# Gates and branches of two hybrid layers with the weights as the moving operand, and five places where work is reordered

## The chip, the cores and the metric

One core of a Trainium2 chip runs the whole program in one launch. The metric is the device time in microseconds (us) of one execution, as a median of several runs. Lower is better.

## What is computed

256 tokens of width 1024 go through a first block (mixer with attention, a recurrent unit and a memory; then a layer of 16,384 experts) and through two hybrid layers. All weights are float32. The part of a hybrid layer that the change rewrites is this:

```python
h = rms_norm(x, norm1_g)
z = h @ w_in
za, zb, zc, zd, zg = jnp.split(z, IN_SPLITS, axis=-1)
ya = retention(za, ret_gn_g)
yb = conformer_conv(zb, conv_w, conv_b, conv_ln_g, conv_ln_b)
yc = spatial_gating(zc, gmlp_ln_g, gmlp_ln_b, gmlp_ws, gmlp_bs)
yd = swa_attention(zd, swa_q_g, swa_k_g, swa_sinks, rel_bias)
ys = jnp.stack([ya, yb, yc, yd], axis=2)
branches = jnp.einsum('bsnc,ncd->bsnd', ys, w_branch)      # 4 branches, 512 -> 1024
gates = jax.nn.sigmoid(zg.reshape(B, S, 4, D_MODEL))       # 1024 -> 4096
mix = jnp.sum(gates * branches, axis=2)
x = x + mix @ w_out
```

## The kernel before

**Stream of weights.** Every weight matrix is cut into units of 512 KB (128 partitions x 1024 float32). SyncE loads them in one fixed order into three raw slots. For each unit ScalarE makes a rounded high half (`hi`, L1181) and GpSimd (two halves of 512 columns, L2606) or VectorE (L1777) makes the remainder, the low half. In most of the program seven units of eight are GpSimd's; in the expert layer's second half, around `w_out` and in the feed-forward VectorE makes all. Four split slots hold the results, so `hi` of unit n may start when TensorE is done with unit n-4. A float32 product is three TensorE passes: high x high, high x low, low x high (`mm3`, L568 to L570).

**Two forms of a unit.** `fm_unit` (L601) gives features by tokens: the weights are the stationary operand (128x128) and the 256 tokens move, so a unit is 24 matmuls of 128x256. `tm_unit` (L628) gives tokens by features: 128 tokens are stationary and 512 weight columns move, so a unit is 12 matmuls of 128x512. The gates and branches are `fm_unit`, `w_out` is `tm_unit`.

**PSUM.** Eight banks: three stream banks that `fm_unit` takes in rotation, and five side banks (`SIDE` is 3) for everything else.

**Order.** Each engine's program is written in rounds: a `main` generator yields once per unit, and after each of its steps the `sides` (convolution, spatial gating, retention, window attention) are stepped once, in the order of a list. Each engine executes its instructions in order. In a hybrid layer `main` does the projections, the 32 gate units, then 16 branch units in the branch order 0, 1, 3, 2, then `project_out` with the 8 units of `w_out`. While gates run, the convolution's normalisation, the spatial gating, and the eight window heads are done on VectorE and ScalarE between them. The sums over branches (L2530, L2531) lie in `gates2`, features by tokens, which is the layout `w_out` needs for its stationary operand: ScalarE and VectorE make its high and low halves (`mix_hi` L1228, `mix_lo` L1830) straight from `gates2`.

**Expert layer.** 128 units of `peer_u` produce one row of expert activations each; 128 units of `peer_v` use them, each with a high and low half of one expert row (`expert_pair`, three of them in rotation, in the space of `h2T`). So that `h2T` is free, the first pair waits for the last `peer_u` matmul. SyncE reloads the residual `X` in four pieces between the first loads of `peer_v`.

**Start.** The memory's values `vm` (4 units, `tm_unit`) use two side banks, which the normalisation of x uses too: its transposes (L689) alternate with the units.

Of the kernel before, what the change touches and what calls it, by code (L numbers as in the profile page):

```python
# [265 lines left out]
class Kernel:  # L266
# [130 lines left out]

    def peer_tiles(self, phase):
# [10 lines left out]
        self.epair = [self.pair(f"expert_pair{i}", [P, TOKENS], at=hot + i * 2048) for i in range(3)]  # L409
        self.g_final = self.place("g_final", [P, D], at=hot + 8192)  # L410
# [30 lines left out]
    def layer_tiles(self, phase):  # L441
# [26 lines left out]
        self.gates2 = self.place("gates2", [P, 32, TOKENS])  # L468
# [82 lines left out]
def pe_program(k):  # L551
# [76 lines left out]
    def tm_unit(key, i, lhs, first, chunks, width, banks, start, stop, ready=None):  # L628
# [5 lines left out]
        for c in range(chunks):  # L634
            if ready is not None:
                pe.wait_ge(*ready(first + c))
            for t, h in ends:
                last = mm3(banks[t][h][:, 0:wd], lhs.at(lambda x: x[:, first + c, t * P:(t + 1) * P]),
# [12 lines left out]
    def close_banks(key, units, lhs_of, ready_of, banks):  # L651
# [19 lines left out]
        at.unit = U[key, units - 1] + 1  # L671

# [44 lines left out]
    def token_major(key, units, chunks, width, lhs, ready=None):  # L717
        banks = [[take(SIDE + t, (key, t))] for t in range(TILES)]
# [32 lines left out]
    def project_out(key, lhs, ready, turns=iter(())):  # L751

        for half in range(2):
            banks = [[take(SIDE + 2 * half + t, (key, half, t))] for t in range(TILES)]
            for u in range(4):
                tm_unit(key, half * 4 + u, lhs, 2 * u, 2, 512, banks, u == 0, u == 3, ready if half == 0 else None)
                if half == 1 and u in (1, 2):
                    next(turns, None)
# [11 lines left out]
    def mixer():  # L770
# [78 lines left out]
        def main():  # L849
# [5 lines left out]
            yield from token_major("vm", 4, 2, 512, k.memT)  # L855
# [30 lines left out]
    def peer():  # L886
# [47 lines left out]
        pe.wait_ge(k.sem("unit_gated"), units_gated(KEYS - 1))  # L934
        for j in range(KEYS - CLOSING):
            ep = k.epair[j % 3]
            pe.wait_ge(k.sem("expert_lo"), j + 1)
            one = ep.at(lambda x: x[:, :].unsqueeze(1))
            tm_unit("peer_v", j, one, 0, 1, 1024, banks, j == 0, False)
        close_banks("peer_v", KEYS, lambda j: k.epair[j % 3], lambda j: (k.sem("expert_lo"), j + 1), banks)  # L940

    def layer(l):
# [17 lines left out]
        def convolution():  # L960
# [24 lines left out]
            for i in range(KM):  # L985
# [12 lines left out]
        def gating():  # L998
            while not at.reached(name("gu"), KM - 1) or name("conv_stats") not in at.stages:
                yield  # L1000
            for i in range(KM):
# [10 lines left out]
                last.then_inc(k.sem("gating_mm"), 1)  # L1012
                yield
# [73 lines left out]

        def main():
# [1886 lines left out]
```

## Time and profile before

| | us |
|---|---|
| median of 3 runs (2141.98 to 2144.8) | 2142.35 |
| the profiled execution's own time | 2145.49 |
| its span, first to last instruction | 2144.2 |
| TensorE busy | 2113.1 (99%) |
| weight loads of TensorE busy | 1958.1 (91%) |
| VectorE / ScalarE / GpSimd busy | 1395.7 / 1247.4 / 977.1 |
| mean granted TensorE clock | 0.998 of full speed |

Around the span lie 1.3 us (2145.49 less 2144.2). TensorE's busy times overlap each other, because matmuls are pipelined: a matmul's own duration is longer than the distance to the next one. The distance between starts is the cost.

### The profile page before, as it was taken

Reading aid. Unit: us, or ns where it says so; the run is one execution under the profiler, and the core shown is the slowest. Engines: PE = TensorE matmul, PEld = TensorE weight load, DVE = VectorE, ACT = ScalarE, POOL = GpSimd, SP = SyncE. Lnnn points to the kernel's source line nnn. Section 1 sums busy time; section 2 is a strip of 40 time slices with the busy share of each in tenths; the row PEclk is TensorE's granted clock in tenths of the full one; section 3 lists DMA queues with packets and bytes.
Section 4 is the critical chain, followed back from the end, with each engine's and each line's share of the span. In section 5 each row is a group of like instructions: output and inputs, shape, how many; then the busy total and the mean of one; then the engine's idle time right before and its main releaser. Section 6 shows DMA issues by size and latency. Waiting matters only on the chain.

```text
span 2144.2 us, 37243 instructions
## 1 busy us (share of the span) xinstructions
PE 2113.1 (99%) x14292; PEld 1958.1 (91%) x14292; DVE 1395.7 (65%) x2706; ACT 1247.4 (58%) x2272; POOL 977.1 (46%) x791
## 2 busy tenths in 40 slices
PE   7999999999999999999999999999999999999999
PEld 7999989999999998888889899998888999998887
DVE  4467655998676756666667765557764864757874
ACT  5669454546777865455445465746555465756553
POOL 4776557999667650000004785660001876661000
PEclk9999999999999999999999999999999999999999
DMA  6444565655444456666665554555565645455565
GB/s 231 149 138 129 172 197 173 196 178 180 145 140 147 141 168 204 195 192 192 195 195 196 186 157 139 155 180 167 187 205 158 189 146 168 141 165 177 187 194 160
DMA packets 103952, 370.59 MB, mean 173 GB/s; under 512 B 11480, under 2 KB 12896, under 8 KB 103264
## 3 DMA queue, kind: packets, MB, share of 16 engines
q1 hardware_dynamic: 103776, 368.21, 54.8%
q8 instruction: 115, 1.88, 0.4%
q14 instruction: 61, 0.50, 0.1%
HBM read 366.05 MB, written 2.11 MB: 172 GB/s over the span
## 4 chain that ended last, share of the span: by engine, by line
PE 88%; DVE 6%; ACT 2%; POOL 1%; issue 1%; DMA 1%; SPq 0%; DVEq 0%; ACTq 0%; POOLq 0%
PE stream_bank L568 14%; PE stream_bank L570 14%; PE stream_bank L569 14%; PE side_bank L568 9%; PE side_bank L570 9%; PE side_bank L569 9%; PE side_bank L577 4%; PE stream_bank L577 4%; PE side_bank L574 2%; PE stream_bank L574 2%; PE side_bank L918 1%; PE side_bank L917 1%; POOL unit_lo L2606 1%; ACT unit_hi L1181 1%; PE side_bank L746 1%
## 5 line engine op out<-in xcount | busy, mean ns | idle before, releaser
L2606 POOL TENSOR_TENSOR unit_lo<-raw,unit_hi 128x512 fp32r<-128x512 f32 (+1 forms) x724 | 938.5, 1324 | 943.6 <-ACT unit_hi L1181 941.6
L1181 ACT ACTIVATE unit_hi<-raw 128x1024 fp32r<-128x1024 f32 (+1 forms) x678 | 708.9, 1046 | 199.5 <-PE side_bank L570 66.0
L1777 DVE TENSOR_TENSOR unit_lo<-raw,unit_hi 128x1024 fp32r<-128x1024 f32 (+1 forms) x316 | 390.3, 1236 | 227.9 <-ACT unit_hi L1181 225.9
L568 PE MATMUL stream_bank<-hT,unit_hi 128*128 128x256 f32 x1360 | 398.9, 293 | 1.8 <-POOL unit_lo L2606 1.8
L570 PE MATMUL stream_bank<-hT,unit_lo 128*128 128x256 f32 x1360 | 384.6, 283 | 0.0
L569 PE MATMUL stream_bank<-hT,unit_hi 128*128 128x256 f32 x1360 | 384.5, 283 | 0.0
L568 PE MATMUL stream_bank<-h2T,unit_hi 128*128 128x256 f32 x1024 | 293.3, 286 | 0.0
L570 PE MATMUL stream_bank<-h2T,unit_lo 128*128 128x256 f32 x1024 | 289.8, 283 | 0.0
L569 PE MATMUL stream_bank<-h2T,unit_hi 128*128 128x256 f32 x1024 | 289.6, 283 | 0.0
L568 PEld LDWEIGHTS stream_bank<-hT,unit_hi 128*128 128x128 f32 x1360 | 259.9, 191 | 3.6 <-POOL unit_lo L2606 2.0
L569 PEld LDWEIGHTS stream_bank<-hT,unit_hi 128*128 128x128 f32 x1360 | 260.0, 191 | 1.6
L570 PEld LDWEIGHTS stream_bank<-hT,unit_lo 128*128 128x128 f32 x1360 | 259.8, 191 | 0.0
L568 PE MATMUL side_bank<-unit_hi,expert_pair 128*128 128x512 f32 x512 | 200.0, 391 | 2.1 <-DVE experts L2238 2.1
L569 PE MATMUL side_bank<-unit_lo,expert_pair 128*128 128x512 f32 x512 | 199.8, 390 | 0.0
L570 PE MATMUL side_bank<-unit_hi,expert_pair 128*128 128x512 f32 x512 | 199.7, 390 | 0.0
L568 PEld LDWEIGHTS stream_bank<-h2T,unit_hi 128*128 128x128 f32 x1024 | 196.6, 192 | 0.0
L569 PEld LDWEIGHTS stream_bank<-h2T,unit_hi 128*128 128x128 f32 x1024 | 196.6, 192 | 0.0
L570 PEld LDWEIGHTS stream_bank<-h2T,unit_lo 128*128 128x128 f32 x1024 | 196.3, 192 | 0.0
L1228 ACT ACTIVATE expert_pair<-experts 128x256 fp32r<-128x256 f32 x128 | 53.4, 418 | 173.3 <-PE side_bank L570 170.8
L577 PE MATMUL side_bank<-sumT,unit_hi 128*128 128x512 f32 x384 | 134.1, 397 | 0.2
L2318 DVE SCALAR_TENSOR_TENSOR side_bank<-conv_in,cols,side_bank 128x256 f32<-128x256 f32 x232 | 113.2, 488 | 6.9
L568 PEld LDWEIGHTS side_bank<-unit_hi,expert_pair 128*128 128x128 f32 x512 | 96.5, 188 | 22.4 <-issue 2.2
(392 smaller groups left out, 4303.9 us busy)
## 6 DMA issues: line engine op xcount, KB each, us to landing
raw<-in_peer_u_dram SPq DMA_DIRECT2D x128, 512.0 KB, 3.5
raw<-in_peer_v_dram SPq DMA_DIRECT2D x128, 512.0 KB, 4.1
raw<-in_gate_dram SPq DMA_DIRECT2D x64, 512.0 KB, 3.5
raw<-in_gt_dram SPq DMA_DIRECT2D x44, 512.0 KB, 3.5
raw<-in_up_dram SPq DMA_DIRECT2D x44, 512.0 KB, 3.5
raw<-in_ffn_out_dram SPq DMA_DIRECT2D x44, 512.0 KB, 3.5
raw<-in_branch_dram SPq DMA_DIRECT2D x32, 512.0 KB, 3.5
raw<-in_w_gate_dram SPq DMA_DIRECT2D x24, 512.0 KB, 3.5
```

The source lines that it names most:

```text
L568: mm(out, l.hi, r.hi, start=start, stop=False)
L569: mm(out, l.hi, r.lo, start=False, stop=False)
L570: return mm(out, l.lo, r.hi, start=False, stop=stop)
L574: low = lambda: mm(bank[:, 0:TOKENS], w.lo, r.hi[:, c, :], start=False, stop=False, skip_group_check=True)
L577: last = mm(bank[:, :].rearrange("p (a t) -> p a t", a=2), w.hi, r.both[:, :, c, :], start=start, stop=stop, skip_group_check=True)
L746: last = mm(bank[:, a:a + n], s.v(kt), s.PT[:, kt * TOKENS + a:kt * TOKENS + a + n], start=(i == 0), stop=(i == len(order) - 1), skip_grou ...
L917: mm(out, first[:, j, :], second[:, j, 0, :], start=True, stop=False)
L1181: activation(k.unit_hi[n % SPLIT_SLOTS][:, 0:w], k.raw[n % RAW_SLOTS][:, 0:w], ACT.Copy).then_inc(k.sem("unit_hi"), 1)
L1228: activation(dst, src, ACT.Copy, scale=scale).then_inc(k.sem(sem), 1)
L1777: V.tensor_tensor(k.unit_lo[s][:, 0:w], k.raw[n % RAW_SLOTS][:, 0:w], k.unit_hi[s][:, 0:w], ALU.subtract).then_inc(unit_lo, 1)
L2318: own.then(V.scalar_tensor_tensor(sums, k.cu[:, i, j:j + TOKENS], w(j), sums, ALU.mult, ALU.add))
L2606: last = G.tensor_tensor(k.unit_lo[s][:, cols], k.raw[n % RAW_SLOTS][:, cols], k.unit_hi[s][:, cols], ALU.subtract)
```

## The change

It does six things; line numbers of the changed kernel are some 100 higher.

1. Gates and branches become `block_unit`: activations stationary, 512 weight columns moving. A block (4 gate units, 2 branch units) fills two stream banks, one for each 128 tokens. ScalarE evicts each bank of a gate block once, 128x512; `add_branch` adds each half branch with the same two VectorE instructions per bank as before.
2. The sums are now tokens by features, so `turn_merged` transposes them on TensorE (16 transposes of 128x128 a layer, in two groups of 8: inside the last branch and behind the first unit of `w_out`), and ScalarE and VectorE make the halves from PSUM (`merged_hi`, `merged_lo`).
3. In the layers VectorE's retention steps come ahead of the convolution's in each round, the window heads last.
4. The convolution's low halves are put two rounds later, and the gating's steps are three rounds apart, not two.
5. `vm` takes stream banks.
6. The first expert pair lies in the space of `X`, so it does not wait for the last `peer_u` matmul; TensorE waits for the last expert's gate only ahead of the second half of `peer_v` unit 0; the reload of `X` waits for `peer_v` unit 0.

```diff
+    def block_unit(key, block, units, u, lhs, banks):
+        i = block * units + u
+        n = U[key, i]
+        w = unit(n)
+        for t in range(TILES):
+            if u == 0:
+                banks.append(take(rotation[turn[0] % len(rotation)], (key, "block", block, t)))
+                turn[0] += 1
+            for c in range(2):
+                last = mm3(banks[t][:, :], lhs.at(lambda x: x[:, 2 * u + c, t * P:(t + 1) * P]),
+                           w.at(lambda x: x[:, c * 512:(c + 1) * 512]), u == 0 and c == 0, u == units - 1 and c == 1)
...
+    def turn_merged(label, x, half, ready):
+        for k2 in (2 * half, 2 * half + 1):
+            bank = take(SIDE + 2 + k2 % 2, (label, k2))
...
+                for t in range(TILES):
+                    last = nc.tensor.transpose(bank[:, j * TOKENS + t * P:j * TOKENS + (t + 1) * P],
+                                               x[:, t, c * P:(c + 1) * P], k.ident)
...
-            yield from token_major("vm", 4, 2, 512, k.memT)
+            yield from token_major("vm", 4, 2, 512, k.memT, in_stream=True)
...
-        pe.wait_ge(k.sem("unit_gated"), units_gated(KEYS - 1))
         for j in range(KEYS - CLOSING):
-            ep = k.epair[j % 3]
+            ep = k.expert_pair(j)
...
+            late = (k.sem("unit_gated"), units_gated(KEYS - 1)) if j == 0 else None
...
-            for i in range(32):
-                fm_unit(name("gate"), i, k.hT2, KD)
-                yield
+            for block in range(8):
+                banks = []
+                for u in range(4):
+                    block_unit(name("gate"), block, 4, u, k.hT2, banks)
+                    yield
...
-                for i in range(KD // 2):
-                    fm_unit(name("branch"), n * KD // 2 + i, part, KM, 2)
-                    yield
+                for half in range(2):
+                    banks = []
+                    for u in range(2):
+                        block_unit(name("branch"), 2 * n + half, 2, u, part, banks)
+                        if n == BRANCH_ORDER[-1] and half and u == 0:
+                            turn_merged(name("merged"), merged, 0, summed())
+                        yield
...
         def expert_hi(j):
             if j == 0:
-                act.wait_ge(unit_mm, U["peer_u", KEYS - 1] + 1)
+                act.wait_ge(k.sem("gates_mm"), 2 * GROUPS)
                 act.wait_ge(*k.over["gates", GROUPS - 1])
             if j == 1:
+                act.wait_ge(unit_mm, U["peer_u", KEYS - 1] + 1)
...
-        at.run(main(), [bias_tables() if l == 0 else iter(()), own_channels(), sides()])
+        at.run(main(), [bias_tables() if l == 0 else iter(()), at.finished(name("branch0"), retention()),
+                        own_channels(), window_heads()])
...
     sp.wait_ge(k.sem("landed_x_out"), 16 * 2 * TILES)
+    sp.wait_ge(k.sem("unit_mm"), U["peer_v", 0] + 1)
```

VectorE in the first hybrid layer, at the first retention head's normalisation, before. `conv_in` rows are taps of the convolution, `ret_n` is what TensorE's transposes at L1056 wait for.

```order
L2425 TENSOR_SCALAR smalls_52<-smalls_52 128x2 [waits dve_own]
L2318 SCALAR_TENSOR_TENSOR side_bank<-conv_in_144,cols_49,side_bank 128x256
L2318 SCALAR_TENSOR_TENSOR side_bank<-conv_in_144,cols_49,side_bank 128x256 [waits dve_own] x3
L1777 TENSOR_TENSOR unit_lo_14_62<-raw_7_55,unit_hi_10_58 128x1024 [waits unit_hi,dve_own]
L2318 SCALAR_TENSOR_TENSOR side_bank<-conv_in_144,cols_49,side_bank 128x256
L2318 SCALAR_TENSOR_TENSOR side_bank<-conv_in_144,cols_49,side_bank 128x256 [waits dve_own] x3
L2431 RECIPROCAL smalls_52<-smalls_52 128x2 [waits ret_root,dve_own]
L2433 TENSOR_SCALAR ret_n_160<-side_bank,smalls_52 128x128 [waits dve_own]
L2433 TENSOR_SCALAR ret_n_160<-side_bank,smalls_52 128x128
L2410 TENSOR_TENSOR S_105_153<-side_bank,layer_consts_134 128x256 [waits ret_scored]
L2411 TENSOR_TENSOR S_105_153<-side_bank,layer_consts_134 128x128
```

The same place of the changed kernel.

```order
L2507 TENSOR_SCALAR smalls_52<-smalls_52 128x2 [waits dve_own]
L2394 SCALAR_TENSOR_TENSOR side_bank<-conv_in_145,cols_49,side_bank 128x256
L2394 SCALAR_TENSOR_TENSOR side_bank<-conv_in_145,cols_49,side_bank 128x256 [waits dve_own] x7
L1851 TENSOR_TENSOR unit_lo_14_62<-raw_7_55,unit_hi_10_58 128x1024 [waits unit_hi,dve_own]
L2513 RECIPROCAL smalls_52<-smalls_52 128x2 [waits ret_root]
L2515 TENSOR_SCALAR ret_n_161<-side_bank,smalls_52 128x128 [waits dve_own]
L2515 TENSOR_SCALAR ret_n_161<-side_bank,smalls_52 128x128
L2492 TENSOR_TENSOR S_106_154<-side_bank,layer_consts_135 128x256 [waits ret_scored]
L2493 TENSOR_TENSOR S_106_154<-side_bank,layer_consts_135 128x128
```

Of the eight taps that stood on both sides of the low half of a weight unit, all now stand ahead of it, and nothing stands between it and the `ret_n` rows.

TensorE at the end of the last branch and the beginning of `w_out`, before (`ys` are the branches' inputs, `hT` the merged rows' halves).

```order
L568 MATMUL stream_bank<-ys_139,unit_hi_13_61 128x256
L569 MATMUL stream_bank<-ys_139,unit_hi_13_61 128x256
L570 MATMUL stream_bank<-ys_139,unit_lo_17_65 128x256
L568 MATMUL stream_bank<-ys_139,unit_hi_13_61 128x256
L569 MATMUL stream_bank<-ys_139,unit_hi_13_61 128x256
L570 MATMUL stream_bank<-ys_139,unit_lo_17_65 128x256
L568 MATMUL side_bank<-unit_hi_10_58,hT_88_136 128x512 [waits unit_lo_pool,mix_lo,bank_free4,bank_free3]
L569 MATMUL side_bank<-unit_lo_14_62,hT_88_136 128x512
L570 MATMUL side_bank<-unit_hi_10_58,hT_88_136 128x512
```

The first unit of `w_out` in the changed kernel, from its seventh matmul on, and the second group of transposes (`gates` are the merged rows, L708 is in `turn_merged`).

```order
L572 MATMUL side_bank<-unit_hi_10_58,hT_89_137 128x512 [waits bank_free5]
L573 MATMUL side_bank<-unit_lo_14_62,hT_89_137 128x512
L574 MATMUL side_bank<-unit_hi_10_58,hT_89_137 128x512
L572 MATMUL side_bank<-unit_hi_10_58,hT_89_137 128x512
L573 MATMUL side_bank<-unit_lo_14_62,hT_89_137 128x512
L574 MATMUL side_bank<-unit_hi_10_58,hT_89_137 128x512
L708 MATMUL side_bank<-base_consts_50,gates_104_152 128x128 [waits bank_free2,bank_free1,bank_free5]
L708 MATMUL side_bank<-base_consts_50,gates_104_152 128x128 x3
L708 MATMUL side_bank<-base_consts_50,gates_104_152 128x128 [waits bank_free2,bank_free1,bank_free6]
L708 MATMUL side_bank<-base_consts_50,gates_104_152 128x128 x3
L572 MATMUL side_bank<-unit_hi_11_59,hT_89_137 128x512 [waits bank_free6,unit_lo_pool]
L573 MATMUL side_bank<-unit_lo_15_63,hT_89_137 128x512
```

Before, `w_out` follows the branch with no other matmul between; now eight transposes stand behind its first unit, and they wait for the sums of the last half branch (bank_free1, bank_free2) and for the low halves made from the first group (bank_free5, bank_free6).

SyncE at the first loads of `peer_v` (raw) and the reload of X, before.

```order
L2747 DMA raw_8_56<-in_peer_v_dram 128x1024 [waits unit_lo_pool]
L2747 DMA raw_9_57<-in_peer_v_dram 128x1024 [waits unit_lo_pool]
L2757 DMA X_53<-x_scratch 128x512 [waits landed_x_out,gates_mm]
L2747 DMA raw_7_55<-in_peer_v_dram 128x1024 [waits unit_lo_pool]
L2757 DMA X_53<-x_scratch 128x512
L2747 DMA raw_8_56<-in_peer_v_dram 128x1024 [waits unit_lo_pool]
```

The same of the changed kernel.

```order
L2846 DMA raw_8_56<-in_peer_v_dram 128x1024 [waits unit_lo_pool]
L2846 DMA raw_9_57<-in_peer_v_dram 128x1024 [waits unit_lo_pool]
L2856 DMA X_53<-x_scratch 128x512 [waits unit_mm,landed_x_out,gates_mm]
L2846 DMA raw_7_55<-in_peer_v_dram 128x1024 [waits unit_lo_pool]
L2856 DMA X_53<-x_scratch 128x512
L2846 DMA raw_8_56<-in_peer_v_dram 128x1024 [waits unit_lo_pool]
```

The order is the same; the first reload of X has one more wait (unit_mm), and the load of the fifth unit of `peer_v` stands right behind it.

## Rows read from the trace of the kernel before

**Rows 1.** Page, part 1: busy us (share of span) xinstructions of each engine

```profile
PE 2113.1 (99%) x14292; PEld 1958.1 (91%) x14292; DVE 1395.7 (65%) x2706; ACT 1247.4 (58%) x2272; POOL 977.1 (46%) x791
```

**Rows 2.** Waits of TensorE: who for whom, us in total, times, longest

```profile
PE side_bank L1056 <- DVE S L2411: 2.9, 2, 1.4
...
PE side_bank L1008 <- DVE gmlp_u L2377: 2.1, 2, 1.1
PE side_bank L568 <- DVE experts L2238: 2.1, 1, 2.1
PE side_bank L568 <- issue: 1.9, 1, 1.9
PE side_bank L728 <- issue: 1.6, 2, 0.8
PE side_bank L568 <- ACT vm L1372: 1.5, 1, 1.5
```

**Rows 3.** Timeline of TensorE, last branch and `w_out`: start, us

```profile
1403.84 0.36 PE L568 MATMUL stream_bank<-ys,unit_hi 128*128 128x256 f32 x1
...
1432.71 0.40 PE L568 MATMUL side_bank<-unit_hi,hT 128*128 128x512 f32 x1
...
1449.07 0.60 PE L691 MATMUL side_bank<-base_consts,X 128*128 128x128 f32 x4
...
1452.27 0.60 PE L691 MATMUL side_bank<-base_consts,X 128*128 128x128 f32 x4
```

**Rows 4.** Timeline of VectorE in the branches

```profile
1418.58 0.69 DVE L2530 SCALAR_TENSOR_TENSOR stream_bank<-gates,stream_bank 128x512 f32<-128x512 f32 x1 [1.53 <-PE stream_bank L570]
1419.31 0.69 DVE L2531 TENSOR_TENSOR gates<-gates,stream_bank 128x512 f32<-128x512 f32 x1
```

**Rows 5.** Timeline of ScalarE in the branches

```profile
1425.79 0.63 ACT L1228 ACTIVATE hT<-gates 128x512 fp32r<-128x512 f32 x1 [3.28 <-DVE gates L2531]
```

**Rows 6.** GpSimd's groups with their shapes, gates and branches of layer 0

```profile
L2606 POOL TENSOR_TENSOR unit_lo<-raw,unit_hi 128x512 fp32r<-128x512 f32 x76 | 98.1, 1315 | 51.9 <-ACT unit_hi L1181 51.6
```

**Rows 7.** Timeline of VectorE around the first retention head

```profile
1221.30 1.23 DVE L1777 TENSOR_TENSOR unit_lo<-raw,unit_hi 128x1024 fp32r<-128x1024 f32 x1 [3.40 <-ACT unit_hi L1181]
1222.44 2.06 DVE L2318 SCALAR_TENSOR_TENSOR side_bank<-conv_in,cols,side_bank 128x256 f32<-128x256 f32 x4
...
1225.72 0.28 DVE L2411 TENSOR_TENSOR S<-side_bank,layer_consts 128x128 f32<-128x128 f32 x1
```

**Rows 8.** Timeline of TensorE at the same place

```profile
1226.05 0.44 PE L1056 MATMUL side_bank<-base_consts,ret_n 128*128 128x128 f32 x2 [1.44 <-DVE S L2411]
```

**Rows 9.** Timeline of VectorE in the gates, first and last of its unbroken stretch

```profile
1318.26 1.75 DVE L2341 RECIPROCAL t2b<-t2b 128x256 f32<-128x256 f32 x1 [7.46 <-ACT t2b L1564]
...
1342.93 0.41 DVE L2377 TENSOR_TENSOR gmlp_u<-side_bank,gmlp_u 128x256 f32<-128x256 f32 x1
```

**Rows 10.** Timeline of TensorE at the start

```profile
30.89 0.47 PE L568 MATMUL side_bank<-unit_hi,memT 128*128 128x512 f32 x1 [1.89 <-issue]
...
69.08 0.39 PE L568 MATMUL stream_bank<-hT,unit_hi 128*128 128x256 f32 x1 [1.76 <-POOL unit_lo L2606]
```

**Rows 11.** Timeline of VectorE at the start

```profile
41.80 0.27 DVE L1942 MEMSET rope_s<- 128x256 f32 x1
```

**Rows 12.** Windows: stretch, its us, busy (instructions) of PE, PEld, DVE, ACT, POOL, PEclk, DMA share, GB/s

```profile
31.50:35.00 3.50, 3.50 (x10) 2.72 (x9) 0.00 (x0) 0.00 (x0) 2.56 (x3) 0.51 0.98 342
...
789.20:792.70 3.50, 3.43 (x8) 2.78 (x9) 1.98 (x3) 1.41 (x3) 0.00 (x0) 0.51 0.75 228
```

**Rows 13.** Timeline of TensorE at the start of `peer_v`

```profile
789.27 0.77 PE L568 MATMUL side_bank<-unit_hi,expert_pair 128*128 128x512 f32 x1 [2.05 <-DVE experts L2238]
```

**Rows 14.** Timeline of SyncE's issues there: start, us to issue

```profile
785.48 0.33 SPq L2747 DMA_DIRECT2D raw<-in_peer_v_dram  x1
```

**Rows 15.** Page, part 6: DMA issues, KB each, median us to landing

```profile
raw<-in_peer_v_dram SPq DMA_DIRECT2D x128, 512.0 KB, 4.1
```

**Rows 16.** Page, part 5: ScalarE's high halves, all of the program

```profile
L1181 ACT ACTIVATE unit_hi<-raw 128x1024 fp32r<-128x1024 f32 (+1 forms) x678 | 708.9, 1046 | 199.5 <-PE side_bank L570 66.0
```

More of the change, by code:

```diff
@@ L626, in halves_unit, with tm_unit @@
         at.unit = n + 1
-    def tm_unit(key, i, lhs, first, chunks, width, banks, start, stop, ready=None):
+    def tm_unit(key, i, lhs, first, chunks, width, banks, start, stop, ready=None, late=None):
         n = U[key, i]
@@ L715, in chunks_of, with token_major @@
         return lambda c: k.over[name, c // 2]
-    def token_major(key, units, chunks, width, lhs, ready=None):
-        banks = [[take(SIDE + t, (key, t))] for t in range(TILES)]
+    def token_major(key, units, chunks, width, lhs, ready=None, in_stream=False):
+        if in_stream:
+            banks = [[take(rotation[(turn[0] + t) % len(rotation)], (key, t))] for t in range(TILES)]
+            turn[0] += TILES
+        else:
+            banks = [[take(SIDE + t, (key, t))] for t in range(TILES)]
         for u in range(units):
@@ L984, in convolution @@
             yield
[L985 removed]
+            for i in range(KM + 1):
                 yield
@@ L1086, in swa @@
                 head(s, [(k.sem("swa_scaled"), 5 * l + 2 + s.column), k.over[name("sv"), 1]]) for s in heads])
+        merged = k.gates2[:, :, BRANCH_ORDER[0] * D:(BRANCH_ORDER[0] + 1) * D]
+        last_branch = lambda half, t: (name("branch"), "block", 2 * BRANCH_ORDER[-1] + half, t)
+        summed = lambda: {2 * h + t: k.over[last_branch(h, t)] for h in range(2) for t in range(TILES)
+                          if last_branch(h, t) in k.over}
         def main():
@@ L1691, in main @@
             for i in range(32):
-                evict(name("gate"), i, k.gates2[:, i, :], ACT.Tanh, scale=0.5)
+                advance(name("gate"), i)
+                if i % 4 == 3:
+                    for t in range(TILES):
+                        label = (name("gate"), "block", i // 4, t)
+                        act.wait_ge(*k.mm_done[label])
+                        activation(k.gates2[:, t, i // 4 * 512:(i // 4 + 1) * 512], k.bank[k.bank_of[label]][:, :], ACT.Tanh,
+                                   scale=0.5).then_inc(k.free[k.bank_of[label]], 1)
                 yield
@@ L1872, in add_out @@
                 advance(key, half * 4 + u)
+                if half == 0 and u == 0 and behind_first is not None:
+                    behind_first()
                 if half == 1 and u in (1, 2):
@@ new lines, in main, with add_branch @@
+                for i in range(KD // 2):
+                    advance(name("branch"), n * KD // 2 + i)
+                    if i % 2:
+                        add_branch(place, n, i // 2)
+                    yield
+        def add_branch(place, n, half):
+            for t in range(TILES):
+                if place == BRANCHES2 - 1 and half:
+                    merged_lo(t)
+                label = (name("branch"), "block", 2 * n + half, t)
+                b = k.bank_of[label]
+                bank = k.bank[b][:, :]
+                gate = k.gates2[:, t, n * D + half * 512:n * D + (half + 1) * 512]
+                first = BRANCH_ORDER[0] * D + half * 512
+                total = k.gates2[:, t, first:first + 512]
+                if place == 0:
+                    dve.wait_ge(*k.over[name("gate"), "block", 2 * n + half, t])
+                dve.wait_ge(*k.mm_done[label])
+                if place == 0:
+                    V.scalar_tensor_tensor(gate, gate, 1.0, bank, ALU.add, ALU.mult).then_inc(k.free[b], 1)
+                    dve.wait_ge(*k.over[label])
+                else:
+                    own.then(V.scalar_tensor_tensor(bank, gate, 1.0, bank, ALU.add, ALU.mult))
+                    V.tensor_tensor(total, total, bank, ALU.add).then_inc(k.free[b], 1)
+                    dve.wait_ge(*k.over[label])
```

114 lines of the change are left out of this document (69 added, 45 removed).

## The prediction

> **What bounds the kernel now.** I read the page first: TensorE is busy 99% of the span, VectorE 65%, ScalarE 58%, GpSimd 46% [rows 1]. So a change pays by what it takes off TensorE's own sequence, or by a wait of TensorE that it removes. The waits of TensorE are few, and six of its lines lie at places that the diff touches: together 12.1 us [rows 2]. Then the timeline, for the distance between starts. A matmul's own duration cannot be summed, since they overlap.
>
> **Gates and branches.** Between the two starts at 1403.84 and 1432.71 us stand 10 branch units, 240 matmuls of 128x256, with nothing between: 28.87 us, 120.3 ns each, 2.887 us a unit. From there to 1449.07 stand six units of w_out, 72 matmuls of 128x512: 16.36 us, 227.2 ns each, 2.727 us a unit [rows 3]. So one matmul of 512 columns costs 13.4 ns less than two of 256. A layer has 48 gate and branch units, so 1152 matmuls of 128x256 become 576 of 128x512. For two layers 2304 x 120.3 ns = 277.2 us becomes 1152 x 227.2 ns = 261.7 us: **-15.4 us**. The six units of w_out are exactly the new form (activations stationary, 512 weight columns moving), so I take the row as it is. Its weakness: there VectorE made the low halves of the weights, here mostly GpSimd.
>
> The Trainium skill ("TensorE: Matmul & The Clock Gate", section "Back-to-back issue gap") would make this term smaller. It gives the isolated gap of a warm matmul as its columns at 2.4 GHz plus about 2.5 ns. By that two of 256 against one of 512 differ by one fixed cost, about 2.6 ns with its rounding, and the term would be an estimated -3.0 us. The distances 120.3 and 227.2 ns of this trace are both larger than the page's 109 and 216, the first by more, so the trace does not agree with it, and the sum goes by the trace. The same section's sustained 131 ns for 512 columns isn't seen here either.
>
> What must keep up at 2.727 us a unit: GpSimd's low halves take 2 x 1.315 = 2.63 us a unit, and it waited 51.9 us in the gates and branches of one layer for the high halves [rows 6], which follow TensorE's pace. Seven units in eight are its own, so it needs 2.30 us per unit on average. It is hidden, with three units made ahead as cushion. The eviction of gates and the sums of branches come in lumps: two banks of three are held by a block, and the next block needs the third at once, the first of the two half a unit after the block's end. The sums take 0.69 + 0.69 us a bank [rows 4]; a bank's first half is complete 1.36 us before the other, so they end some 0.1 and 1.5 us after the block, and the freed banks are asked for 1.4 and 5.5 us after it. I cost this at nothing; if the cover were gone, it would be up to 1.4 us for each of 16 half branches.
>
> **Transposes of the merged rows.** Four groups of 8 over both layers. Four transposes in w_out stretch the unit after 1449.07 to 3.20 us (start of one L691 to the next) against 2.73, so 0.47 for four, 0.94 for eight [rows 3]: **+3.8 us**. The second group waits for the last sums. Call A the end of the last branch's first half. Its second half ends at A + 2 x 2.73 + 0.94 = A + 6.4, the first w_out unit at A + 9.1. VectorE has from A + 5.0 on (first bank full) two sums of 1.4 and two `merged_lo` of about 0.7 (as rows 4), which makes A + 9.0 if the first of them starts at A + 4.8; ScalarE's halves are 0.63 each [rows 5]. That is only 0.1 under the point where TensorE arrives, so I put 0.3 a layer: **+0.6 us**. Bounds 0 and 2 x 1.4 (one sum late).
>
> **Retention ahead of the convolution.** TensorE waits 1.44 us in each layer at L1056 for VectorE [rows 2, 8]. VectorE had stood idle for 3.40 us, made a weight unit's low half, then four taps in 2.06 us, and only then the `ret_n` rows and the score products that TensorE waited for, until 1226.0 [rows 7]. The changed order has all taps ahead of the low half, in what was idle. Without the four taps VectorE is done 2.06 earlier, at 1223.9, ahead of TensorE's arrival (1226.05 - 1.44 = 1224.6), so the wait goes: -2.9, and some 0.1 of restart at each: **-3.1 us**. Bounds: 0 (taps late in their turn delay another step) and -3.2.
>
> **Convolution and gating steps.** The two waits at L728 and L1008 are 1.6 + 2.1 = 3.7 us for both layers [rows 2]. VectorE works without a break from 1318.26 to 1343.34 [rows 9], after 7.46 us in which it waited for ScalarE's square root. The edit changes the order in that stretch, not its 25 us of work, and by its end TensorE will have done 11 gate units that are each 0.16 us shorter, so it comes 1.75 us sooner. What VectorE orders first (the window heads' queries) comes in time; the gating products at the end then come late. I think that the first wait goes and the second grows to nearly what both were: **-0.5 us**. Bounds: -3.7 when both go, and +3.5 when TensorE's 1.75 us are given back in each layer.
>
> **vm in stream banks.** The wait of 1.89 us before vm's second step is for a bank that the normalisation's halves still hold [rows 10]; in stream banks it goes. Behind it the granted clock was at the lower of its two levels (1.2 GHz) for 3.5 us, after TensorE had stood: 10 matmuls there, against 3.5 / 0.227 = 15 at the upper one, so 3.5 - 2.27 = 1.2 us [rows 12]. It shouldn't fall without the gap. Then the wait for the eviction of vm (1.5 us, rows 2) goes too, since va's banks are free. But 20 us later TensorE waits 1.76 us for a low half of GpSimd [rows 10], and GpSimd had been held up by small operations that hang on VectorE's rope tables from 41.80 on [rows 11]. That chain begins behind the last normalisation step, which moves only by the 1.9 + 1.2 us ahead of it. What TensorE gains beyond it is waited out at 69 us: **-3.1 us**. Bounds: -1.9 and -4.6 (with the 1.5).
>
> **First expert pair.** TensorE waits 2.05 us at 789.27 for VectorE [rows 13], in a chain from the last `peer_u` matmul by ScalarE's and VectorE's halves. The changed kernel makes the first pair before that matmul. The clock behind it was at the lower level as well: 8 matmuls in 3.5 us instead of 1.82 [rows 12]. 2.05 + 1.68 = **-3.7 us**. The price is on SyncE: the reload of X waits for `peer_v` unit 0 (789.27 - 2.05 + 2.73 = 789.9), and the load of the fifth unit, issued at 785.48 before [rows 14], stands behind it. Issued at 790.3 and landing 4.1 us later [rows 15] it is there at 794.4; high and low half take 1.05 [rows 16] and 1.23 [rows 7], so 796.7; TensorE needs it at 787.2 + 4 x 2.73 = 798.1. I cost it at nothing, with 1.4 us of cover; bounds of the whole part 0 and -3.8.
>
> **Sum.** -15.4 + 3.8 + 0.6 - 3.1 - 0.5 - 3.1 - 3.7 = -21.4 us. The profiled execution took 2145.49, 3.1 over the median, and would take 2124.1; the median 2142.35 becomes **2121 us**.
>
> **Rivals.**
> - The waits in the gates all vanish and vm's reach their full bound: -3.2 - 1.5 more, 2116. For it: VectorE stands idle for 7.46 us ahead of its stretch, and the square root that opens it stood behind an eviction of a gate that comes only every fourth unit now. Against: VectorE's unbroken 25 us [rows 9]. 0.15.
> - VectorE is the bound in the gates and takes back what TensorE gains there: +4 to +8, 2125 to 2129. For it: the same row, and the window heads that follow in the same queue. Against: behind that stretch TensorE has enough gates left that no side waits. 0.14.
> - The reload of X doesn't hide: landing takes longer with two more transfers beside it, and TensorE waits for `peer_v`'s fifth unit; a wait of 2 to 4 us, perhaps with the clock falling again: 2124 to 2127. Against: 1.4 us of cover. 0.06.
> - The form of the matmul gives little: 13.4 ns is a matter of where w_out's and the branches' operands lie, and the gap follows a fixed cost per instruction of some 2 to 3 ns: the term is -3, the time 2133. This is the Trainium skill's rule above. Against it stand both distances in one trace, 0.2 us apart in place. 0.03.
> - Slower. GpSimd becomes the bound of the 96 gate and branch units: with 7 of 8 units its own, the gain of 21.4 us (0.223 a unit) is gone when a unit takes 2.95 us, that is 3.37 for a unit of GpSimd, 1.69 a half against the 1.315 shown. At 1.8 a half: 3.15 a unit, +40 for the two layers, 2162. For it: evictions and sums now come in lumps beside it. Against: a mean of 1.315 over 76 instructions amid the same VectorE work [rows 6]. 0.04.
>
> **How the numbers follow.** The forecast itself has 0.58; its own range, by its bounds, is 2117 to 2125. The range **2112 to 2131** takes in the first three rivals and leaves out the last two and the ends of some bounds. A measurement tells 0.2%, 4.3 us, from no change. All cases but the last are faster by more than that; a bit of it goes to no change, where several bounds meet: faster 0.93, same 0.03, slower 0.04.
>
> **What would show it.** Right: a gate or branch unit at 2.73 us; 16 transposes a layer, with no wait over 0.5 at the second group; no wait at the `ret_n` transposes; TensorE's clock at the upper level at 31 and 788 us; `peer_v` starting within 0.2 us of the last `peer_u` matmul; one wait of 1 to 2 us left in each layer's gates, at a window head's transposes or the gating's products; a wait for GpSimd left near 65 us. Wrong: a distance of 235 ns or more between 512-column matmuls, TensorE waiting for `unit_lo` of GpSimd in many gate units, or for stream banks at the blocks' beginnings, or for the raw slot of the fifth `peer_v` unit.

## The result and the profile after

Median of four runs 2128.29 us (2126.46 to 2128.98) against 2143.57 of before (four runs): ratio 0.9926, 95% interval 0.9913 to 0.9939, 15.3 us faster. Five more runs of the same kernel (experiment `again`) gave 2129.81, so that all nine have a median of 2128.7. Forecast were 2121 and 21.4 us. The two profiled executions differ by 19.0 us, 2126.46 against 2145.49 us, and the spans as well:

The page of the changed kernel, its first lines (compare [rows 1]):

```profile
span 2125.2 us, 34923 instructions
PE 2100.6 (99%) x13172; PEld 1898.4 (89%) x13172; DVE 1394.9 (66%) x2706; ACT 1244.3 (59%) x2240; POOL 979.4 (46%) x791
```

TensorE has 1120 instructions less (1152 fewer matmuls, 32 transposes more) and is busy as before. Its waits, against [rows 2]:

```profile
PE stream_bank L572 <- POOL unit_lo L2705: 5.2, 5, 2.2
PE side_bank L780 <- ACT S L1305: 4.7, 2, 2.3
...
PE side_bank L572 <- DVE first_expert_pair L2320: 0.4, 1, 0.4
```

The six lines that the diff touched are gone from this list, but for 0.4 us at the first pair. In their place stand two new ones: 2.3 us in each layer at the transposes of the first window head (L780), and a longer wait for GpSimd's low halves at the start.

The form, on TensorE's timeline at the end of the last branch (compare [rows 3]):

```profile
1390.24 0.47 PE L572 MATMUL stream_bank<-unit_hi,ys 128*128 128x512 f32 x1
...
1414.93 1.03 PE L708 MATMUL side_bank<-base_consts,gates 128*128 128x128 f32 x8
1415.72 0.49 PE L572 MATMUL stream_bank<-unit_hi,ys 128*128 128x512 f32 x1
1416.05 0.40 PE L573 MATMUL stream_bank<-unit_lo,ys 128*128 128x512 f32 x1
...
1418.59 0.39 PE L572 MATMUL side_bank<-unit_hi,hT 128*128 128x512 f32 x1
...
1421.32 1.03 PE L708 MATMUL side_bank<-base_consts,gates 128*128 128x128 f32 x8
1422.11 0.48 PE L572 MATMUL side_bank<-unit_hi,hT 128*128 128x512 f32 x1
```

From 1390.24 to 1414.93 stand nine branch units with nothing between: 24.69 us, 2.74 a unit, with one restart in it. The undisturbed w_out unit from 1418.59 to 1421.32 takes 2.73 us. A group of eight transposes takes 0.79 us to the next start, and the unit behind it 2.87 (1415.72 to 1418.59) instead of 2.73: 0.93 a group. No row has a wait at the second group.

From the starts of the stages in both timelines (layer 0; the differences of layer 1 agree within 0.04 us):

| stage | before | after | difference |
|---|---|---|---|
| layer's norm to the first gate unit | 126.79 | 124.84 | -1.95 |
| 32 gates, with heads and gating between | 113.52 | 109.79 | -3.73 |
| 16 branch units (after: with one group of transposes) | 49.17 | 47.98 | -1.19 |
| w_out | 22.76 | 23.62 | +0.86 |

That is 6.0 us a layer, and 11.8 from the first layer's norm to the end of the second layer. The start up to the unit of 69.08 / 64.16 us gave 4.9 (1.1 of it in the first transfers, which have nothing to do with the change), the first pair 1.7 and the clock behind it 1.6; some 0.9 are lost again between 64 and 780 us.

### The profile page after: what moved, and what is told of

Read it like the earlier page. It is cut to its first block, busy times and chain, and to the rows that moved or that the text cites. A ratio compares the mean times of both kernels' runs of the same rounds, so it can differ in the third digit from the quotient of the medians.

```text
span 2125.2 us, 34923 instructions
## 1 busy us (share of the span) xinstructions
PE 2100.6 (99%) x13172; PEld 1898.4 (89%) x13172; DVE 1394.9 (66%) x2706; ACT 1244.3 (59%) x2240; POOL 979.4 (46%) x791
## 4 chain that ended last, share of the span: by engine, by line
PE 89%; DVE 6%; ACT 2%; POOL 1%; DMA 1%; issue 1%; SPq 0%; ACTq 0%; DVEq 0%; POOLq 0%
PE stream_bank L572 14%; PE stream_bank L574 14%; PE stream_bank L573 14%; PE side_bank L572 9%; PE side_bank L574 9%; PE side_bank L573 9%; PE side_bank L581 4%; PE stream_bank L581 4%; PE side_bank L578 2%; PE stream_bank L578 2%; PE side_bank L963 1%; PE side_bank L962 1%; POOL unit_lo L2705 1%; PE side_bank L789 1%; ACT unit_hi L1239 1%
## 5 line engine op out<-in xcount | busy, mean ns | idle before, releaser
L572 PE MATMUL stream_bank<-hT,unit_hi 128*128 128x256 f32 x848 | 248.6, 293 | 3.1 <-POOL unit_lo L2705 3.1
L574 PE MATMUL stream_bank<-hT,unit_lo 128*128 128x256 f32 x848 | 239.8, 283 | 0.0
L573 PE MATMUL stream_bank<-hT,unit_hi 128*128 128x256 f32 x848 | 239.7, 283 | 0.0
L572 PE MATMUL side_bank<-unit_hi,expert_pair 128*128 128x512 f32 x508 | 197.7, 389 | 0.0
L574 PE MATMUL side_bank<-unit_hi,expert_pair 128*128 128x512 f32 x508 | 197.7, 389 | 0.0
L572 PEld LDWEIGHTS stream_bank<-hT,unit_hi 128*128 128x128 f32 x848 | 162.3, 191 | 4.5 <-POOL unit_lo L2705 3.5
L573 PEld LDWEIGHTS stream_bank<-hT,unit_hi 128*128 128x128 f32 x848 | 162.3, 191 | 0.9
L574 PEld LDWEIGHTS stream_bank<-hT,unit_lo 128*128 128x128 f32 x848 | 162.2, 191 | 0.0
```

What stands on the lines that cost most here:

```text
L572: mm(out, l.hi, r.hi, start=start, stop=False)
L573: mm(out, l.hi, r.lo, start=False, stop=False)
L574: return mm(out, l.lo, r.hi, start=False, stop=stop)
```

## The experiments

Differences to the changed kernel are to its median of nine runs, 2128.7. `again` repeats it. The nine lie between 2126.5 and 2131.2, so a difference of 2 to 3 us between two medians is hardly clear of the noise. The stages of the profiles tell more. Here is the time from the first gate unit's start to the first branch unit's, in us; a star marks a layer in which the granted clock fell to its lower level in this stage.

| kernel | layer 0 | layer 1 |
|---|---|---|
| changed kernel | 109.79 | 109.78 |
| again | 109.79 | 111.32* |
| form_only | 111.31* | 111.42* |
| steps_undone | 109.81 | 111.15* |
| act_heads_first | 114.52* | 113.85* |
| turn_later (branches 1.9 longer) | 108.73 | 108.75 |
| pool_gates | 109.12 | 109.09 |
| gating_late | 108.50 | 108.50 |

**again.** 

> The changed kernel unaltered, run again beside before. The timed medians differ by 15.3 us, the two profiled executions by 19.0. If the profile of the changed kernel was merely a quick execution, the difference comes out at 15 to 17 us again and the new profile's span lies 1 to 2.5 us above 2125.2, with the excess in places that do not belong to the change (the first transfers, waits for a transfer). If the profile is typical and the timed runs were not, it comes out at 18 to 20.

2129.81 us (2126.9 to 2131.15), ratio 0.9937 (0.9924 to 0.9951); before 2143.47 in 16 runs. The difference was 15.3 us in the first comparison and is 13.7 here, under both ranges expected; and this profile is again of a quick execution, 2126.9 us. The 19.0 of the two profiles came of an execution 1.8 us under its median beside one 2 to 3 over its own. Where executions differ is shown below under the clock.

**form_only.** The retention order, the convolution and gating steps, vm's banks and the first pair as before.

> Only the 512-column form and the transposes that it needs; the other four changes (retention order, convolution and gating steps, vm's banks, first expert pair) are undone. By the terms of the prediction 15.4 - 3.8 - 0.6, so 11 us faster than before. By the stages of the two profiles (gates -3.75, branches -1.2, w_out +0.9 in a layer) only about 8. Where VectorE bounds the gates, 7.5 or less, and the waits in the gates grow over the 3.7 us of before.

2137.36 us (ratio 0.9975, 0.9966 to 0.9984): 6.1 faster than before, where the terms said 11. Its waits of TensorE in the gates:

```profile
PE stream_bank L572 <- ACT gates L1756: 5.1, 2, 2.6
```

ScalarE ahead of that wait's end (1333.29), in layer 0:

```profile
1330.76 0.60 ACT L1628 ACTIVATE conv_out<-conv_out,cols 128x256 f32<-128x256 f32 x1 [1.96 <-DVE conv_out L2418]
...
1332.66 1.06 ACT L1756 ACTIVATE gates<-stream_bank 128x512 f32<-128x512 f32 x2
```

The row of TensorE is a wait that I had costed at nothing, "evictions come in lumps": the next block's bank waits for ScalarE to evict a gate block, and ScalarE, in order, stands at work that VectorE has not yet released. It is 2.6 us a layer where before had 0.8 and 1.0 [rows 2]. That makes 1.4 of the 5 us that are missing; 3 are restarts, counted below. In the profile the clock fell behind this wait in both layers; how much of the rest that is can't be read from one profile.

**steps_undone.** Only the convolution's and the gating's steps as before:

```diff
-            for i in range(KM + 1):
+            for i in range(KM):
                 yield
...
                 last.then_inc(k.sem("gating_mm"), 1)
                 yield
                 yield
-                yield
```

and the matching steps on ScalarE and VectorE. 

> The changed kernel with the convolution's and the gating's steps as before. If the stretch is bounded by VectorE's 25 us of work, the order matters little: within 1.5 us of the changed kernel, with waits of 3 to 6 us over both layers left at the heads' transposes or the gating. If these steps were what removed the two waits of before, it is 3.7 us slower. If they are what made the new wait of 2.3 us a layer, it is 2 to 4 us faster.

2131.08 us, 2.4 slower, but its five runs (2126.3 to 2132.33) take in all nine of the changed kernel, so the time shows no difference. The eviction's wait of 2.6 us a layer is back and the 2.3 at the transposes is gone: one wait for another of like size. The gates of layer 0 take 109.81 us against 109.79, so the steps are worth nothing; in layer 1, and near 64 us, the clock fell.

**act_heads_first.**

```diff
-        at.run(main(), [bias_tables() if l == 0 else iter(()), own_channels(), sides()])
+        at.run(main(), [bias_tables() if l == 0 else iter(()), sides(), own_channels()])
```

on ScalarE. 

> The changed kernel with ScalarE stepping the window heads ahead of the convolution and gating in each round. In the profile the wait of 2.3 us a layer at the first head's transposes ends with ScalarE's normalisation of that head, which stands behind the rounding of the gating's first product, itself waiting for VectorE; the head's reciprocal was ready 2.6 us earlier. If the order on ScalarE is the cause, the wait shrinks to about 1.1 and the kernel is 2.4 us faster than the changed one. If VectorE bounds the stretch, the wait reappears at the gating or the next head and the time stays.

2136.56 us, 7.9 slower. Both theories fell: the wait grew to 3.5 us a layer, and one of 0.7 came before it at the scores. Together that is 3.6 us more for both layers; in the profile, 10.6 us longer than the changed kernel's, the clock also fell behind both waits and near 64 us. From TensorE's waits in this kernel (line, for whom, us in total, times, longest):

```profile
PE side_bank L780 <- ACT S L1305: 6.9, 2, 3.5
...
PE side_bank L771 <- issue: 1.4, 2, 0.7
```

**turn_later.**

```diff
-        for _ in range(5):
+        for _ in range(5 if s.bias is None else 6):
             yield
```

on TensorE, with a step more on ScalarE and VectorE. 

> The changed kernel with the transposes of each window head, and what follows from them, one round later on TensorE, ScalarE and VectorE. If the wait of 2.3 us a layer is only the first head's normalisation coming one round late, it goes: 4.7 to 5 us faster than the changed kernel, and up to 2.5 more in executions in which the clock would have fallen behind these waits, so 2122 to 2124. If VectorE's and ScalarE's work bounds the stretch, a wait of about the same length comes back at the next head or the gating or a stream bank, and the time stays within 1.5 us of 2128.7.

2129.39 us, no gain. The wait at L780 went, and 2.0 us for GpSimd's low half and 1.0 us for VectorE's branch sums came in each layer. The gates end 1.1 us sooner, the branches take 1.9 longer. So four orders of the same work leave 2.3 to 4.2 us of waits a layer. None ends them, which points to VectorE and ScalarE as the bound there; but the order is not indifferent, as `act_heads_first` and `gating_late` show.

**vm_side.**

```diff
-            yield from token_major("vm", 4, 2, 512, k.memT, in_stream=True)
+            yield from token_major("vm", 4, 2, 512, k.memT)
```

> The changed kernel with vm in the side banks again. If vm's new banks gave the 3.8 us that the two profiles show up to 64 us, this is 3 to 4 us slower than the changed kernel's 2128.7 (median of its nine runs). If what TensorE gained there is waited out at the low halves of GpSimd, which hang on VectorE's tables, the wait near 64 us (2.2 in the changed kernel) is 0.5 or so shorter here and the loss is 2 us or less. If the clock falls behind the gap of 1.9 us in only some executions, runs differ by about 1.4 us and the loss has two levels.

2131.05 us (2129.8 to 2135.6), 2.3 slower. The gap of 1.89 us is back at 30.62 and the wait near 68 is 1.73 (2.17 in the changed kernel): between the two theories. In the profile, of the slowest execution, the clock fell behind the gap, and 3.8 us are lost between 20 and 70 us.

**pair_undone.** The first expert pair in `h2T`'s space, its waits and SyncE's as before. 

> The changed kernel with the first expert pair made as before. The gap of 2.05 us at the start of peer_v comes back for the 0.4 of the changed kernel: 1.7 us slower where the clock stays up behind the gap, 3.2 where it falls as in the profile of before. The prediction had 3.7.

2133.37 us, 4.7 slower, more than either figure expected; the gap of 2.06 is back. In the profile the clock fell behind it, and the two cost 3.2 us between 780 and 800 us.

**dve_order.** VectorE's convolution steps ahead of the retention's. 

> The changed kernel with VectorE's convolution steps ahead of the retention's again. The wait at the ret_n transposes comes back: 1.6 us a layer with the restart, and 0.2 at the next head, 3.1 to 3.9 us in all, unless the order in the gates changes with it, which can give or take 2 us.

2133.95 us, 5.2 slower, over the 3.9 expected. By the profile the retention costs 1.94 us more in each layer, 3.9 in both. TensorE's waits in this kernel have the row of [rows 2] again, with the same size:

```profile
PE side_bank L1102 <- DVE S L2493: 2.9, 2, 1.4
```

**later_spread.** turn_later, and in GpSimd's `tables`:

```diff
-                if i % 3 == 0:
-                    yield
+                yield
```

> As turn_later, and GpSimd's small table operations in the first stage one pair a round instead of three, so that the low halves near 58 and 64 us come in time. If these operations are what the two waits there hang on (1.0 and 2.2 us in the changed kernel), 2 to 3.5 us faster than turn_later. If the transfers or the normalisation's chain bound that stretch, within 1 us of turn_later.

2128.78 us, 0.6 faster than turn_later, within the noise. The waits at 58 and 64 us shrank from 1.0 and 2.3 to 0.3 and nothing, 3.0 us at 108 us, but waits for low halves at 240 to 290 us took half back: 1.3 were left at 348 us.

**pool_gates.** In the assignment of the low halves:

```diff
+            if any(U[f"gate.{l}", 0] + 8 <= n < U[f"gate.{l}", 0] + 28 for l in range(LAYERS)):
+                by = "pool"
```

> The changed kernel with the low halves of gate units 8 to 27 all on GpSimd, so that VectorE loses one of 1.22 us inside its unbroken stretch in each layer. If VectorE's amount of work sets the wait at the first head's transposes, it falls from 2.3 to 1.1 us a layer, the clock no longer falls behind it, and the kernel is 2.4 to 4 us faster than the changed one (2128.7). If GpSimd's additional work slows VectorE's products of two SBUF operands (0.42 us alone, 1.4 to 1.5 beside GpSimd in the profile), the wait stays over 2 us.

2126.26 us (2125.64 to 2127.23), 2.4 faster. The wait fell from 2.34 to 1.70 us a layer, about half of the 1.22 us that one low half takes VectorE; that is 1.3 us for both layers, and where the rest of the 2.4 lies is not shown. VectorE's stretch from the first reciprocal to the gating product became only 0.68 us shorter, 27.49 us (1307.36 to 1334.85) against 28.17 (1305.18 to 1333.35). Rows of this kernel, VectorE's timeline and then GpSimd's at the same time:

```profile
1321.77 1.52 DVE L2428 TENSOR_TENSOR ys<-conv_out,ys 128x256 fp32r<-128x256 f32 x1
...
1324.98 0.99 DVE L2544 SCALAR_TENSOR_TENSOR swa_q<-swa_q,cols,swa_var 128x256 f32<-128x256 f32 x1
...
1327.33 0.41 DVE L2428 TENSOR_TENSOR ys<-conv_out,ys 128x256 fp32r<-128x256 f32 x1
```

```profile
1321.45 5.67 POOL L2707 TENSOR_TENSOR unit_lo<-raw,unit_hi 128x512 fp32r<-128x512 f32 x4 [0.96 <-ACT unit_hi L1241]
1333.61 2.53 POOL L2707 TENSOR_TENSOR unit_lo<-raw,unit_hi 128x512 fp32r<-128x512 f32 x2 [6.48 <-ACT unit_hi L1241]
```

The same product takes 1.52 us while GpSimd makes low halves (until 1327.12) and 0.41 behind them, while GpSimd does nothing. The changed kernel has the 1.5 and the 0.4 at other products, with no net change; but the scaling at 1324.98 took 0.55 there, and those 0.44 us are most of what is missing. GpSimd was at work beside it in both kernels. Its low half and the scaling, first in the changed kernel, then in this one (the third of the four):

```profile
1322.92 1.29 POOL L2705 TENSOR_TENSOR unit_lo<-raw,unit_hi 128x512 fp32r<-128x512 f32 x1 [0.96 <-ACT unit_hi L1239]
1323.95 0.55 DVE L2542 SCALAR_TENSOR_TENSOR swa_q<-swa_q,cols,swa_var 128x256 f32<-128x256 f32 x1
```

```profile
1324.41 1.29 POOL L2707 TENSOR_TENSOR unit_lo<-raw,unit_hi 128x512 fp32r<-128x512 f32 x1
1324.98 0.99 DVE L2544 SCALAR_TENSOR_TENSOR swa_q<-swa_q,cols,swa_var 128x256 f32<-128x256 f32 x1
```

In both the scaling ends 0.3 us behind the low half; here it began earlier in it. So VectorE pays for the rest of GpSimd's running instruction, and the price hangs on where in it the product begins. That GpSimd's additional work brought the worse place is argued, not shown. The Trainium skill ("GPSIMD Engine Reference", "Specifications") says that the SBUF interfaces are shared with VectorE, with contention for instructions of two SBUF inputs; the trace agrees, and gives the price.

**pool_spread.** pool_gates with the spread tables. 

> As pool_gates, with GpSimd's table operations spread at the start as in later_spread, which ended the two waits near 58 and 64 us there (3.5 us, of which 1.3 were left at 348 us). Expected 1 to 3 us faster than pool_gates, with no wait over 1.5 us between 20 us and the end and no lower clock behind one.

2122.98 us (2120.8 to 2123.84, four runs), ratio to before 0.9901 (0.9886 to 0.9916): 5.7 faster than the changed kernel and 3.3 faster than pool_gates, and the best here; in its profile the clock fell nowhere from 20 us to the end. Of the waits of TensorE, 1.7 us a layer are left at the window head, more than the expectation had, and up to 1.2 for low halves:

```profile
PE side_bank L782 <- ACT S L1307: 3.4, 2, 1.7
PE stream_bank L574 <- POOL unit_lo L2707: 3.0, 4, 1.2
```

**gating_late.** pool_spread with a step moved from behind `gating_hi` on ScalarE, and from behind `gating_lo` on VectorE, to ahead of it. 

> As pool_spread, and the rounding of each gating product on ScalarE (and its low half on VectorE) one round later, so that the first head's normalisation no longer stands behind it. In pool_spread the wait of 1.70 us a layer ends with that normalisation, which starts 0.3 us behind the rounding of a product that VectorE had just made, while the head's reciprocal was 2.6 us old. If that order on ScalarE is what is left, the wait falls to about 0.6 us a layer: 2 us faster than pool_spread (2123.0), so 2121. If VectorE's work is what is left, the wait moves to another instruction and the time stays within 1 us.

2123.21 us, the same within the noise. The wait at L782 fell to 0.47 us as expected, 0.4 of the gain came back as a wait for a low half one unit later, and there was another of 1.4 us in the first block, which the edit does not touch. The gates take 108.50 us for pool_spread's 109.1, so 1.2 us are gained in both layers; the first block lost 0.7 of them in this profile. TensorE's waits:

```profile
PE stream_bank L574 <- DVE gates L2184: 1.4, 1, 1.4
...
PE side_bank L782 <- ACT S L1307: 0.9, 2, 0.5
```

## Why the prediction held, and which terms were off

The direction, the range and the main term's mechanism held; the size was 6 to 8 us off, the worth of three terms (1, 4 and 7). The time lies outside the forecast's own 2117 to 2125 and among the 2125 to 2129 of the rival in which VectorE takes back 4 to 8 us. It does so by luck: the waits there grew by 0.9 us in all, and most of what is missing is in terms that the rival left alone.

1. **Gates and branches, -15.4 forecast, about -12.4 measured.** The cadence of the new form is the predicted 227 ns where nothing interrupts. The step that failed is "a gate or branch unit at 2.73 us": I priced every unit as an undisturbed one. In a layer the block units stand in 28 stretches between heads, transposes and gating products (26 before). The first unit behind such a place pays a restart: 2.87 us behind the transposes above and 2.96 behind a head's scores instead of 2.73, where before it was 2.97 and 3.06 instead of 2.89. Summed over the gates and branches of a layer, without the waits, the stretches take 5.0 us more than their matmuls at the undisturbed cadence, and 3.4 before: 1.6 us a layer, which the term lacked. The rival in which 512 columns save only a fixed cost of 2 to 3 ns is refuted: undisturbed, 12 matmuls take 2.73 us for 24 in 2.89, now in branch units as well, with the branches' operands. The rule of the Trainium skill that I weighed ("TensorE: Matmul & The Clock Gate", "Back-to-back issue gap") gives an estimated 3.0 us for this term; the trace disagrees by a factor of four.
2. **Transposes, +3.8 and +0.6.** 4 x 0.93 = 3.7, and no wait at the second group. Right.
3. **Retention, -3.1.** Stage -1.95 a layer, -3.9, and 5.2 in the timed undoing. The wait went, and so did a small one at the second head that I had left out.
4. **Convolution and gating, -0.5 forecast, +0.9 measured.** The prediction said that one of the two waits would go and the other grow to nearly the sum. It grew beyond it: 2.34 against 0.83 + 1.04 a layer. The step that failed is "the edit changes the order in that stretch, not its 25 us of work". From the first reciprocal to the first gating product VectorE took 24.67 us before [rows 9] and takes 28.17 now, in both layers; with the old steps (`form_only`, `steps_undone`) it took 24.6, so the steps did it. They put the second head's scores ahead of the gating product, and more of the products beside GpSimd's low halves (twelve products of 128x256 take 10.1 us, 8.4 before). The stretch and the end of its chain in the changed kernel, VectorE, ScalarE and TensorE one after the other:

```profile
1305.18 1.75 DVE L2417 RECIPROCAL t2b<-t2b 128x256 f32<-128x256 f32 x1 [5.23 <-ACT t2b L1624]
...
1331.41 0.60 DVE L1916 SCALAR_TENSOR_TENSOR S<-side_bank,bias 128x128 f32<-128x128 f32 x2
...
1333.35 0.41 DVE L2458 TENSOR_TENSOR gmlp_u<-side_bank,gmlp_u 128x256 f32<-128x256 f32 x1
```

```profile
1333.80 0.42 ACT L1286 ACTIVATE ys<-gmlp_u 128x256 fp32r<-128x256 f32 x1 [0.80 <-DVE gmlp_u L2458]
1334.12 0.79 ACT L1305 ACTIVATE S<-S,smalls 128x128 f32<-128x128 f32 x2
```

```profile
1335.05 0.52 PE L780 MATMUL side_bank<-base_consts,S 128*128 128x128 f32 x3 [2.34 <-ACT S L1305]
```

   VectorE's stretch, begun at 1305.18, ends with the gating product; ScalarE's normalisation of the head stands behind the rounding of that product, and TensorE behind both. The rival "VectorE takes back what TensorE gains there" was the truth of this place, though not in size: in `turn_later` and `steps_undone` the wait moved and kept its size; less work on VectorE (`pool_gates`) made it smaller, and so did a later rounding on ScalarE (`gating_late`).
5. **vm, -3.1.** The profiles give 3.8 without the first transfers, the timed undoing 2.3. The mechanism was right: what TensorE gained was partly waited out, now in two waits of 0.96 and 2.17 us for low halves. That GpSimd's table operations made these was argued, and `later_spread` and `pool_spread` show it. GpSimd's timeline in the changed kernel:

```profile
56.29 2.51 POOL L2705 TENSOR_TENSOR unit_lo<-raw,unit_hi 128x512 fp32r<-128x512 f32 x2
58.76 1.20 POOL L2753 TENSOR_TENSOR smalls<-smalls 128x12 f32<-128x12 f32 x1
60.05 0.24 POOL L2754 TENSOR_SCALAR smalls<-smalls 128x12 f32<-128x12 f32 x1
60.37 0.21 POOL L2753 TENSOR_TENSOR smalls<-smalls 128x12 f32<-128x12 f32 x1
...
61.61 2.50 POOL L2705 TENSOR_TENSOR unit_lo<-raw,unit_hi 128x512 fp32r<-128x512 f32 x2
```

   Each group of six holds the next low half up by 2 to 3 us.
6. **First pair, -3.7.** A wait of 0.4 was left; the profiles give 3.3, the undoing 4.7. The reload of X cost TensorE nothing: SyncE issued it at 786.64, right after `peer_v` unit 0, and the fifth unit's load behind it, and no wait for that unit is in the list.
7. **The clock.** Two terms contained 1.2 and 1.7 us (a fall cost 1.6 at either place) for stretches at the lower level, as if every execution had them and the changed kernel none. That step failed. The granted clock behind the same wait of 2.3 us in layer 1, in `again` and, second row, in the first profile of the changed kernel (columns as [rows 12]):

```profile
1828.00:1832.00 4.00, 3.89 (x12) 3.26 (x13) 2.48 (x7) 3.50 (x10) 4.00 (x4) 0.57 0.55 170
```

```profile
1829.00:1833.00 4.00, 3.86 (x20) 3.32 (x21) 2.51 (x8) 3.53 (x10) 4.00 (x4) 1.00 0.48 160
```

   Twelve matmuls against twenty in 4 us. The new waits have their own chance of a fall, and the old ones did not always have it: in `form_only`, which keeps both gaps of before, the clock stayed up at 29.6 and at 787.5 us.

```profile
29.60:33.00 3.40, 3.40 (x18) 2.88 (x19) 0.00 (x0) 0.09 (x1) 3.29 (x3) 1.00 0.95 348
787.50:791.00 3.50, 3.50 (x16) 2.90 (x17) 2.04 (x4) 1.83 (x5) 0.00 (x0) 1.00 0.67 224
```

The single undoings add up to 14.6 us (2.4, 2.3, 4.7 and 5.2) where undoing all four costs 8.7. By the stages of the profiles there is no such gap. Without the first transfers and without falls of the clock the steps cost 0, vm 2.2, the first pair 1.6 and the retention 3.9: 7.7 us; the same places in `form_only` cost 7.6. In `vm_side` and `pair_undone` a fall of 1.6 us came on top at the place that was undone, in `form_only` at neither. What stays open is how often each wait brings a fall, since there is one profile a kernel, and so how the timed medians divide.

## What to carry to other kernels

A cadence taken from an undisturbed stretch overstates the gain where units are interrupted: count the interruptions and price the first unit behind each. Where TensorE is made faster beside another engine's unbroken stretch, look at that engine's sum of work first; shifting steps moves the wait, and it can lengthen the stretch (24.6 to 28.2 us here), so list what stands ahead of the instruction that others wait for; taking work off that engine shortened it by 0.7. A time that a profile shows for a lower clock belongs to one execution, so count it with a chance, for the waits that vanish as for those that come.

## What the runs showed of the hardware

Whether the granted clock falls to its lower level behind a wait differs from execution to execution. In the profiles here it fell behind 6 of 10 waits of 2.3 us at the window heads' transposes and behind both of 3.5; behind 3 of 4 of the 2.6 us for a gate block's eviction; behind 3 of 8 of those of 2.1 to 2.3 near 64 us; behind none of the eight of 1.7 to 2.0 in the layers of `turn_later`, `later_spread`, `pool_gates` and `pool_spread`. The shorter wait is not safe, though: of the waits of 1.9 to 2.1 near 31 and 788 us it fell behind 4 of 6 (both in the kernel before, one each in `vm_side` and `pair_undone`, none of two in `form_only`). A fall cost 1.3 to 1.6 us: behind the same wait of 2.3 us the gates of a layer took 109.8 us without one and 111.3 to 111.4 with it.

A VectorE product of 128x256 from two SBUF operands took 0.41 to 0.43 us in nearly every case without GpSimd at work, and up to 1.52 beside it. In the changed kernel 44 such products began while GpSimd made a low half: 42 of them ended 0.24 to 0.32 us behind that low half and took 0.55 to 1.52 us; the other two began in its last 0.06 us and took 0.41.
